# A transformer pair on one core: a fourth group of seven products in place of two filler chunks, key halves copied by DMA, and zero halves of the value products left out

## The reference

```python
h = rms_norm(x, norm1_g)
proj = h @ w_in                       # q, k, v (3 x 1024) and bg, cg, xc (3 x 1024)
y_attn = chunked_relpos_attention(q, k, v, q_norm_g, k_norm_g, rel_bias)
y_conv = gated_short_conv(bg, cg, xc, conv_w, conv_b)
gates = sigmoid(h @ w_gate + b_gate)
merged = g_attn * (y_attn @ w_attn_proj) + g_conv * (y_conv @ w_conv_proj)
x = x + merged @ w_out
x = x + square(relu(rms_norm(x, norm2_g) @ w_up)) @ w_down
```

## Time and profile before

| | |
|---|---|
| median of 3 runs | 2145.02 us (2144.67 to 2146.3) |
| the profiled execution | 2145.05 us |
| its span (first to last instruction) | 2143.3 us |
| TensorE busy | 2125.5 us, 99% |
| VectorE busy | 1507.6 us, 70% |
| ScalarE busy | 956.1 us, 45% |
| GpSimd busy | 1007.2 us, 47% |
| granted clock of TensorE | 0.999 of full speed |
| chain of waits that ended last | TensorE 93%, VectorE 3%, GpSimd 1%, ScalarE 1% |

### The profile page before, as it was taken

One profiled execution on the slowest core, in us unless ns is written; L12 is line 12 of the kernel. 1 busy time (PEld: TensorE's weight loads), 2 busy tenths in 40 slices (PEclk: granted clock), 3 DMA queues, 4 the chain that ended last, 5 costly groups with the idle time before them and its releaser, 6 DMA issues.

```text
span 2143.3 us, 28233 instructions
## 1 busy us (share of the span) xinstructions
PE 2125.5 (99%) x10402; PEld 1782.4 (83%) x10402; DVE 1507.6 (70%) x2619; ACT 956.1 (45%) x1714; POOL 1007.2 (47%) x697
## 2 busy tenths in 40 slices
PE   9999999999999999999999999999999999999999
PEld 8888888888888888888888888788878888888887
DVE  6776774354875457878778668433877887898886
ACT  5554524433332256666666522212555455433331
POOL 3232465555555533122131156547566564666564
PEclk9999999999999999999999999999999999999999
DMA  7320114332234253333333166314144435836432
GB/s 233 106 77 21 46 59 177 123 133 79 79 118 156 95 140 89 87 85 110 86 90 105 50 221 235 98 58 183 47 165 157 167 137 187 314 109 236 145 117 111
DMA packets 198439, 269.66 MB, mean 126 GB/s; under 512 B 57944, under 2 KB 116088, under 8 KB 198176
## 3 DMA queue, kind: packets, MB, share of 16 engines
q1 hardware_dynamic: 126992, 205.58, 27.8%
q10 hardware_dynamic: 71312, 62.30, 9.5%
HBM read 191.23 MB, written 85.00 MB: 129 GB/s over the span
## 4 chain that ended last, share of the span: by engine, by line
PE 93%; DVE 3%; POOL 1%; ACT 1%; issue 1%; DMA 1%; DVEq 0%; ACTq 0%; SPq 0%; POOLq 0%
PE ps L205 80%; PE ps L2404 3%; PE ps L2379 3%; PE ps L2391 2%; PE ps L777 1%; PE ps L752 1%; PE ps L763 1%; POOL w_lo L3281 1%; PE ps L2416 1%; DVE a_lo L447 1%; PE ps L687 0%; DMA qk_raw<-qkv_tm 0%; DVE prob L2701 0%; PE ps L2916 0%; PE ps L1478 0%
## 5 line engine op out<-in xcount | busy, mean ns | idle before, releaser
L205 PE MATMUL ps<-a_hi,w_hi 128*128 128x512 f32 x1312 | 507.8, 405 | 2.7 <-DVE a_lo L447 1.2
L160 POOL TENSOR_TENSOR w_hi<-w_raw,zero 128x512 fp32r<-128x512 f32 x156 | 187.7, 1233 | 675.6 <-PE ps L205 562.1
L205 PE MATMUL ps<-a_hi,w_lo 128*128 128x512 f32 x1312 | 490.7, 392 | 0.0
L205 PE MATMUL ps<-a_lo,w_hi 128*128 128x512 f32 x1312 | 488.5, 390 | 0.0
L205 PE MATMUL ps<-w_hi,a_hi 128*128 128x512 f32 (+1 forms) x960 | 369.0, 384 | 3.8 <-POOL w_lo L673 2.0
L205 PE MATMUL ps<-w_hi,a_lo 128*128 128x512 f32 (+1 forms) x960 | 367.4, 383 | 0.0
L205 PE MATMUL ps<-w_lo,a_hi 128*128 128x512 f32 (+1 forms) x960 | 367.0, 382 | 0.0
L205 PEld LDWEIGHTS ps<-a_hi,w_lo 128*128 128x128 f32 x1312 | 246.1, 188 | 54.3
L205 PEld LDWEIGHTS ps<-a_hi,w_hi 128*128 128x128 f32 x1312 | 246.6, 188 | 43.5 <-DVE a_lo L447 2.7
L205 PEld LDWEIGHTS ps<-a_lo,w_hi 128*128 128x128 f32 x1312 | 247.2, 188 | 38.0
L165 POOL TENSOR_TENSOR w_lo<-w_raw,w_hi 128x512 fp32r<-128x512 f32 x156 | 224.1, 1467 | 3.1
(11 more groups left out here) (308 smaller groups left out, 4083.2 us busy)
## 6 DMA issues: line engine op xcount, KB each, us to landing
mlp_part<-u_parts SPq DMA_DIRECT2D x26, 1024.0 KB, 7.3
w_raw<-in_w_in_dram SPq DMA_DIRECT2D x21, 1024.0 KB, 5.3
u_parts<-mlp_acc SPq DMA_DIRECT2D x28, 512.0 KB, 2.8
u_parts<-res SPq DMA_DIRECT2D x28, 512.0 KB, 2.8
feat_fm<-stage ACTq DMA_DIRECT2D x52, 256.0 KB, 2.0
conv_in<-feat_fm ACTq DMA_DIRECT2D x24, 512.0 KB, 5.2
qkv_raw<-in_w_in_dram SPq DMA_DIRECT2D x11, 1024.0 KB, 5.4
res<-in_x_dram SPq DMA_DIRECT2D x16, 512.0 KB, 6.4
```

The lines of the kernel that those rows point to most:

```text
L160: hi = nc.gpsimd.tensor_tensor(w_hi[slot][:, k:k + 2, :], w_raw[:, k:k + 2, :], zero[:, 0:1].unsqueeze(2).to_broadcast([P, 2, CW]), ALU.add)
L205: last = nc.tensor.matmul(out_of(o), lhs, rhs(o), start=first and n == 0, stop=final and n == 2)
```

## The change

The number of groups goes from 3 to 4 and that of filler chunks from 13 to 11 (one ahead of the loop, 40 products inside it). For all heads but the first, ScalarE and VectorE make the key's high and low part on partitions 64-127 only, and a transfer on ScalarE's queue copies each to partitions 0-63 (64 x 512 float32, 128 KB): the high one right behind `k_high` in steps 3 and 7, behind a wait of ScalarE for its own copy; the low one in step 5, and for the second half in step 1 of the next head. `scores` of blocks 0 and 4 wait for these transfers too. `k_low` now stands in steps 4 and 0, and `v_low` moves from step 6 to step 5. A value product whose key block only one of the two query blocks sees takes 128 columns, after those that both see, and the memsets of the zero halves are gone.

```diff
@@ -102,8 +102,8 @@
         W_U1 = seg(io["w_in"], 0, 1792, 2)
         W_OUT1 = seg(io["w_out"], 0, 0, 4, wide=2)
         W_V2 = seg(io["w_in_2"], 0, 2048, 4, wide=2)
-        BCX_GROUPS = 3
-        FILL_CHUNKS = 13
+        BCX_GROUPS = 4
+        FILL_CHUNKS = 11
         W_BCX2 = seg(io["w_in_2"], 0, 3072 + 512 * BCX_GROUPS, 12 - 2 * BCX_GROUPS)
         W_GATE = seg(io["w_gate_2"], 0, 0, 8)
         W_AP = seg(io["w_attn_proj_2"], 0, 0, 4)
@@ -2317,6 +2317,7 @@
                 bias_in = [S("bias_in0"), S("bias_in1")]
                 turned_r, hi_r, lo_r = S("turned_r"), S("hi_r"), S("lo_r")
                 hi_v, lo_v = S("hi_v"), S("lo_v")
+                k_copied = S("k_copied")
                 dve_self = S("dve_sel")
                 scored, shifted, exped, scaled = S("scored"), S("shifted"), S("exped"), S("scaled")
                 turned, hi_p, lo_p = S("turned"), S("hi_p"), S("lo_p")
@@ -2397,13 +2398,15 @@
                         pe.wait_ge(lo_p, i * STEPS + (m + 2))
 
                         pe.wait_ge(o_done, i * 8 + (m // 2 + 1))
-                        first, last_kb = window(2 * g)[0], window(2 * g + 1)[1] - 1
-                        for kb in range(first, last_kb + 1):
+                        even, odd = range(*window(2 * g)), range(*window(2 * g + 1))
+                        both = [(kb, 0, 256) for kb in even if kb in odd]
+                        one = [(kb, 0, P) for kb in even if kb not in odd] + [(kb, P, 256) for kb in odd if kb not in even]
+                        for kb, c0, c1 in both + one:
                             sl = kb - (2 * g - back) + nslot * (m // 2 % 2)
                             for pt in (pt_hi, pt_lo):
-                                last = nc.tensor.matmul(ps[:, O_BANK, 0:256], v_st[:, h, kb, :], pt[:, sl, :],
-                                                        start=(kb == first and pt is pt_hi),
-                                                        stop=(kb == last_kb and pt is pt_lo))
+                                last = nc.tensor.matmul(ps[:, O_BANK, c0:c1], v_st[:, h, kb, :], pt[:, sl, c0:c1],
+                                                        start=((kb, c0, c1) == both[0] and pt is pt_hi),
+                                                        stop=((kb, c0, c1) == one[-1] and pt is pt_lo))
                         last.then_inc(valued, 1)
 
                     def round_(head, r):
@@ -2465,7 +2468,10 @@
                             product_part(i, n, 1)
                             if n + 2 < STEPS or not last:
                                 if (n + 2) % 8 in (0, 4):
-                                    pe.wait_ge(lo_r, i * 4 + (2 * ((n + 2) // 8) + (n + 2) % 8 // 4 + 2))
+                                    head, r = i * 2 + (n + 2) // 8, (n + 2) % 8 // 4
+                                    pe.wait_ge(lo_r, head * 2 + (r + 2))
+                                    if head:
+                                        pe.wait_ge(k_copied, 32 * ((head - 1) * 2 + (r + 1)))
                                 scores(i, n + 2, (n + 2) // 8 % 2)
                             if n % 2 and not (first and n < 2):
                                 values(i, n - 2)
@@ -2493,9 +2499,20 @@
 
                     def k_high(head, slot, r):
                         cols = slice(r * 512, (r + 1) * 512)
-                        for side in (1, 0):
-                            nc.scalar.activation(k_hi[side * HD:(side + 1) * HD, slot, cols],
-                                                 ps[HD:P, T_BANK, :], ACT.Copy, scale=gains[HD:P, 0:1]).then_inc(hi_r, 1)
+                        if head == 0:
+                            nc.scalar.activation(k_hi[0:HD, slot, cols], ps[HD:P, T_BANK, :], ACT.Copy,
+                                                 scale=gains[HD:P, 0:1])
+                        nc.scalar.activation(k_hi[HD:P, slot, cols], ps[HD:P, T_BANK, :], ACT.Copy,
+                                             scale=gains[HD:P, 0:1]).then_inc(hi_r, 1)
+                        if head:
+                            act.wait_ge(hi_r, 2 * (head * 2 + r) + 2)
+                            act.dma_start(k_hi[0:HD, slot, cols].bitcast(F32), k_hi[HD:P, slot, cols].bitcast(F32)).then_inc(k_copied, 16)
+
+                    def copy_k_low(head, slot, r):
+
+                        act.wait_ge(lo_r, head * 2 + (r + 2))
+                        cols = slice(r * 512, (r + 1) * 512)
+                        act.dma_start(k_lo[0:HD, slot, cols].bitcast(F32), k_lo[HD:P, slot, cols].bitcast(F32)).then_inc(k_copied, 16)
 
                     def v_high(head, slot):
                         act.wait_ge(head_in, (head + 1) * 48)
@@ -2591,11 +2608,15 @@
                                     k_high(head, slot, nn // 4)
                                 if nn == 4:
                                     v_high(head, slot)
+                                if nn == 5:
+                                    copy_k_low(head, slot, 0)
                                 if nn == 7 and not last:
 
                                     act.wait_ge(turned_r, 2 * head + 2)
                                     act.wait_ge(lo_v, head + 1)
                                     load_head(i * 2 + (hh + 2))
+                            if n < STEPS and nn == 1 and not (first and n < 8):
+                                copy_k_low(i * 2 + hh, hh % 2, 1)
                     pair_loop(body)
                     out_half(pairs - 1, STEPS - 1)
                     for x in range(FILLED):
@@ -2611,10 +2632,6 @@
                                    (st_h[0], 16), (st_h[1], 16)):
                         dve.sem_inc(s_, n_)
 
-                    for pt in (pt_hi, pt_lo):
-                        for side in range(2):
-                            nc.vector.memset(pt[:, nslot * side + nslot - 1, 0:P].bitcast(F32), 0.0)
-                            nc.vector.memset(pt[:, nslot * side, P:256].bitcast(F32), 0.0)
                     nc.vector.memset(bias[0:HD, :, wmax - HD:wmax], NEG)
                     nc.vector.memset(bias[HD:P, :, 0:HD], NEG)
                     dve.wait_ge(const_in, 32)
@@ -2622,13 +2639,13 @@
                     dve.wait_ge(const_ok, 1)
 
                     def q_low(head, slot, r):
-                        dve.wait_ge(hi_r, 3 * (head * 2 + r) + 1)
+                        dve.wait_ge(hi_r, 2 * (head * 2 + r) + 1)
                         cols = slice(r * 512, (r + 1) * 512)
                         nc.vector.scalar_tensor_tensor(q_st[HD:P, slot, cols], ps[0:HD, T_BANK, :], gains[0:HD, 0:1],
                                                        q_st[0:HD, slot, cols].bitcast(F32), ALU.mult, ALU.subtract)
 
                     def k_low(head, slot, r, side):
-                        dve.wait_ge(hi_r, 3 * (head * 2 + r) + 3)
+                        dve.wait_ge(hi_r, 2 * (head * 2 + r) + 2)
                         cols = slice(r * 512, (r + 1) * 512)
                         ins = nc.vector.scalar_tensor_tensor(k_lo[side * HD:(side + 1) * HD, slot, cols],
                                                              ps[HD:P, T_BANK, :], gains[HD:P, 0:1],
@@ -2704,12 +2721,12 @@
                                 head, slot = i * 2 + (hh + 1), (hh + 1) % 2
                                 if nn in (3, 7):
                                     q_low(head, slot, nn // 4)
-                                if nn in (4, 5):
-                                    k_low(head, slot, 0, nn - 4)
-                                if nn == 6:
+                                if nn == 4:
+                                    k_low(head, slot, 0, 1)
+                                if nn == 5:
                                     v_low(head, slot)
-                            if n < STEPS and nn < 2 and not (first and n < 8):
-                                k_low(i * 2 + hh, hh % 2, 1, nn)
+                            if n < STEPS and nn == 0 and not (first and n < 8):
+                                k_low(i * 2 + hh, hh % 2, 1, 1)
                             low()
                             if n % 2 == 0 and not (first and n < 4):
                                 out_sum(i, n - 3)
```

## The result

| | before | after |
|---|---|---|
| median | 2145.49 us (4 runs, 2144.67 to 2146.3) | 2165.14 us (4 runs, 2163.48 to 2167.28) |
| span of the profiled execution | 2143.3 us | 2163.4 us |
| granted clock of TensorE | 0.999 | 0.999 |

The ratio is 1.0093, with a 95% interval of 1.008 to 1.0106: 20 us slower, where the range ended at 2155. The clock is the same, so it explains nothing. The *loop* runs from the first scores product to the start of the last turn: 456.7 us before, 436.9 after. The *groups* are the pieces of the chain on the group products. Loop and groups together make +19.4 us and leave 0.7 of the 20.1 us of span for all other stages. A loop is read from one profiled execution, and executions of the kernel before lie up to 3.9 us apart (2143.88 to 2147.77), so a loop difference under some 2 us shows little by itself.

The account below looks back on a forecast made before the run. TensorE, busy for 99% of the span, was taken as the bound. Filler -44.8, fourth group +38.4, narrow products -1.9 and waits +7.7 sum to -0.6 us on 2145.05: forecast 2144.5 us, range 2136 to 2155.

Parts of the forecast that it names:

- Filler and fourth group: TensorE: two filler chunks fewer save 44.8 us, a fourth group without gaps adds 38.4 us.
- Narrow products: Value products on TensorE: 192 passes cut from 256 to 128 columns save 1.9 us, ends 1.9 and 11.5.
- Key transfers: ScalarE's queue and scores of blocks 0 and 4: idle time hides wait and issues; cost 0, ends 0 and 30 us.
- late landings: Rival at the scores of blocks 0 and 4: transfers needing 4.4 us cost 30 us, 2175 us; chance 0.05.
- block 0 the tighter place: Low key copy before block 0's scores: about 3.5 us of room once filler is gone, 2.0 us needed.
- Lost cover: Attention: with less filler, TensorE's waits for `pt_lo` come to 10.5 us, 7.7 more than now.
- Turn 3 to 4: Transposes of blocks 3 and 4: VectorE's run holds turn 4 back in 11 heads, 2.2 us lost.
- Turn 4 to 5: Transposes of blocks 4 and 5: 3.4 us needed, 3.45 there in 8 of 14 heads; about even.
- The splits of GpSimd: Beside the attention they slow VectorE's scalings and `v_low` by 1.65 us; a third is lost, 5.5 us.
- VectorE becomes the bound: Rival in steps 3 to 7: 15 us more waits for `pt_lo`, 2151.8 us, up to 2155.5; chance 0.20.
- the waits ... pass 18: Sign of being wrong: TensorE's waits for `pt_lo` stay under 4 us or pass 18.
- near 10 us, spread over blocks 0, 4, 5 and 6: Sign of being right: size and place of TensorE's waits for `pt_lo` in the attention.

Follow-up runs that it names:

- e2: The changed kernel without the key transfers, both key sides made by ScalarE and VectorE as before; 2151.08 us.
- e3: The kernel before with only two constants changed, four groups and eleven filler chunks; 2152.07 us.
- f7: The kernel before with the narrow value products alone, and without the memsets of the zero halves; ratio to before 0.9993.
- e1: The changed kernel with the transfer of the key's high part issued one step later; 2149.94 us.
- g2: The changed kernel with the head loads issued ahead of the wait and the high transfer, in the same step; 2149.09 us.
- g1: The kernel before with only one wait added, for ScalarE's own key copies, ahead of the loads of step 7; 2156.99 us.
- g3: f7 with `v_high` and `v_low` moved to step 2, `v_low` ahead of `pt_lo`; 2161.1 us.
- f6: e1 with GpSimd's split of the filler's weights cut to the first of four pieces; ratio to before 1.0012.
- f8: The changed kernel with filler spread evenly and without the key transfers; ratio to before 0.9999.
- e4: The changed kernel with three groups and thirteen filler chunks again; 2158.92 us.
- h3: h2 with the key transfers, the high one issued a step later as in e1; ratio to before 1.0021.
- h2: f8 with the value parts made in step 2, `v_high` ahead of `q_high` and `v_low` last in VectorE's step; ratio to before 1.0.

## Why the prediction was wrong

**Filler and fourth group: right.** -44.4 us for -44.8. The group cost 39.2 for 38.4. The chain of waits of the kernel after has it:

```profile
399.60 230.55 PE ps L205 x1008
...
630.17 0.70 DVE res L2172
...
631.00 153.79 PE ps L205 x672
```

1680 passes at 0.2288 us, where the earlier trace rows has 1512, and one stop of 0.9 us in between, which "the three present groups run without a gap, so I take the fourth to do so too" missed. With four groups the first product starts on another pair of banks and waits for a sum on VectorE that three groups did not meet. That cause is read from the code and the chain; no run changed the banks.

**Narrow products: right.** -1.4 in e2 against e3, -0.6 in f7, for -1.9. The trace bears out the 0.11 us per pass. The Trainium skill, TensorE: Matmul & The Clock Gate, section Back-to-back issue gap, gives 81 ns for a pass of 128 columns, which would have made 7.5 us (an estimate); no run here shows that. The rule of its section LDWEIGHTS, a load's columns over 1.2 GHz (an estimate of 107 ns for 128 columns), agrees with the 0.11 us.

**Key transfers: the step that failed.** It reads: "that idle time also hides the new self-wait behind `k_high` and four DMA issues of 0.33 us; behind that self-wait only the next `pt_hi` is queued". In step 7 the three loads of the next head but one are queued there too, 2.2 us of issuing (1191.17 to 1193.38 after). ScalarE's 166.9 us of idle time in the earlier trace rows was a total over the stage; in step 7 the reserve was the 1.05 us in brackets at 970.62, against the 2.91 us of queue in brackets at 1193.49. The change took the second key copy away, 0.69 us, and with it the overlap of three issues with copies. The cost is 15.1 us (e1), 16 (g2), against 0 that I took. The interval from 0 to 30 us that I kept for this step was drawn from late landings, and the chance that went with it was 0.05; a queue order wasn't among the cases. The Trainium skill, TensorE: Matmul & The Clock Gate, section Architectural detail: the array is 16× 32×32, not 1× 128×128, says that ScalarE's and VectorE's queues are strictly first in, first out. g1 and g3 agree, with +10.5 us of loop (against before) and +17.4 (against f7) for one wait each.

Landings were as taken in the median, 2.2 and 2.6 us for 2.0, and late twice (2.8 us of waits in all), each issue 0.48 us instead of 0.33. The prediction called block 0 the tighter place; both waits were at block 4, for low transfers of the second half, which are issued in step 1 behind the loads of step 7 and of the bias (median landing 3.0 us, against 2.2 for those issued in step 5). At the first of the two waits a bias load issued at 946.59 lands at 954.06 us, and the low transfer, issued behind it at 947.79, at 954.94. The kernel after, the issues of the low transfer at L2515 (ns, min/median/max), then their landing:

```profile
L2515 ACTq DMA_DIRECT2D k_lo<-k_lo x30: 468/482/515, 825.2 to 1222.4; - x30
...
DMA to landing us min/median/max: 2.2/2.6/7.1
```

**Lost cover: right in kind, too small.** 11.5 us instead of 7.7 (e3). Turn 3 to 4 lost about 5 us and not 2.2 (16 x 0.33 in e1): I had VectorE's run end 2.51 us behind turn 3 and took 0.1 for the handover, where it is 2.57 and 0.15, and in some heads more still; the turn is short of a triple in 13 of 16 heads, where I had counted 11 of 15. Turn 4 to 5, taken as even, lost 3 (16 x 0.20). The list of waits shows only some of it: e3 has 8.0 us there against 2.8, and the loop has lost 11.5. I had read that list as the whole cost. The splits of GpSimd, which I gave 5.5 us, are worth 2.4 at most by f6. Filler in the wrong place is worth 4.5 (e2 against f8). So some 5 to 7 us of the 11.5 are accounted for by a cause that was tried, each by itself and never both together; the rest is spread over turns that follow VectorE, and stays open. The 11.1 us from which the rival "VectorE becomes the bound" was to decide aren't worked out; six tenths of the GpSimd surcharge make 12.1 (5.0 + 9.9 - 2.8).

**The sum** with measured terms, in us of loop and groups: filler -43.7, group +39.2, lost cover +11.5, narrow products -1.4, transfers in a good place -1.3, queue order +15.1; together +19.4, of 19.7 (medians) to 20.1 (spans) measured. The loop terms are differences along one chain of kernels (before, e3, e2, e1, after), so that they add up is no proof; g1, g2 and e4 are what checks the largest. The rival "VectorE becomes the bound", with 2151.8 to 2155.5 us, gives the right sign and would have been about right for e3 (2152.07). It was not what happened to the change: VectorE is less busy after than before, and two thirds of the wait for `pt_lo` (12.1 of 18.1 us) are at block 0, where it passes on ScalarE's delay. What I had written as a sign that I am wrong, "the waits ... pass 18", came near (17.1), while "near 10 us, spread over blocks 0, 4, 5 and 6" holds for e2 (7.8).

## What to carry to other kernels

A wait in an in-order queue costs what stands behind it: list every instruction and every DMA issue between the wait and the next result that another engine is due, and add their durations; if it comes to more than the slack in that very step (not in the stage's average), move the wait behind them or a step later. When a wait's releaser is late, ask what *its* releaser was: here TensorE waited for VectorE, VectorE for ScalarE, and ScalarE for its own issues. Work that fills a schedule is also its slack: taking 43.7 us of it from the loop gave back 32.2.

## What the runs showed of the hardware

- A transfer from 64 partitions to 64 others inside the memory, 128 KB, takes 0.48 us of ScalarE's queue in the median (0.47 to 0.52 in the kernel after), longer than the store of a 128-partition tile of 256 KB (0.33). In the kernel before, instructions on ScalarE ran beside the issues of its queue (key copies from 968.17, load issues 967.50 to 969.53); in g1, with a wait between them, the issues started at 973.25, after the copies had ended.
- It lands in 2.2 us at best, and in up to 7.1 (after) and 7.5 (h3). The Trainium skill, DMA: Bandwidth & Descriptors, section Anatomy of one DMA, gives a fit for transfers that GpSimd issues of 2.0 us and bytes over 436 GB/s, an estimate of 2.3 us for 128 KB. The medians of 2.2 and 2.6 in the kernel after, issued by ScalarE, agree. In g2 the high ones of step 7, issued right behind three head loads, land in 3.9 to 5.2 us but for the last, and the late ones fit no constant; two of them stand for 4.0 us of waits in h3, which is 5.2 us slower than h2.
- From the end of VectorE's `pt_lo` to the start of the transpose that waited for it are 0.14 to 0.15 us at least, in every kernel looked at.
- The first of a run of 128-column passes may seem cheap (0.06 us); the wide one behind the run then starts 0.05 us late.
